# Modulation products of a two-block transformer step: k tiles outside, column groups of the array inside

## The reference

```python
cond_x = jax.nn.silu(c)
cond_c = jax.nn.silu(c_ctx)
for layer in range(DEPTH):
    mx = jnp.split((cond_x @ mod_w[layer] + mod_b[layer])[:, None, :], N_MOD, axis=-1)
    mc = jnp.split(cond_c @ mod_w[layer] + mod_b[layer], N_MOD, axis=-1)
    ...
```

## Time and profile before

| what | value |
|---|---|
| median of 3 runs | 3141.31 us (3138.47 to 3141.94) |
| span of the profiled execution | 3137.4 us |
| PE busy | 2995.0 us, 95% |
| DVE, ACT busy | 1347.2 us (43%), 1218.3 us (39%) |
| modulation products, line 902 | 576 records, 241.4 us together |
| loads of mod_w | 144 of 512 KB |

### The profile page before, as it was taken

The page is one execution under the profiler, slowest core; times in us unless marked ns, Lnnn a source line. Parts: engine busy times, 40 slices in busy tenths (PEclk is TensorE's granted clock), DMA queues, the critical chain, the costliest instruction groups (busy, mean ns, idle before and its releaser), DMA issues.

```text
span 3137.4 us, 44044 instructions
## 1 busy us (share of the span) xinstructions
PE 2995.0 (95%) x16870; PEld 2443.6 (78%) x16870; DVE 1347.2 (43%) x2147; ACT 1218.3 (39%) x1793; POOL 0.6 (0%) x6
## 2 busy tenths in 40 slices
PE   7999999999999999899998999899998999899998
PEld 6734989989338999888886568688876888687998
DVE  5521455556214555633334135433334333365555
ACT  5421635544115355533323234333323332245553
POOL 0000000000000000000000000000000000000000
PEclk9999999999999999999999999999999999999999
DMA  5575554654756455523232111232332223220454
GB/s 177 177 251 194 182 167 149 188 159 136 233 181 214 156 161 184 165 80 102 95 94 81 51 34 59 73 97 94 97 97 74 94 93 98 90 81 1 137 183 136
DMA packets 113830, 401.01 MB, mean 128 GB/s; under 512 B 12353, under 2 KB 15553, under 8 KB 113729
## 3 DMA queue, kind: packets, MB, share of 16 engines
q1 hardware_dynamic: 113728, 399.62, 39.6%
HBM read 398.52 MB, written 1.05 MB: 127 GB/s over the span
## 4 chain that ended last, share of the span: by engine, by line
PE 90%; DVE 4%; ACT 2%; DMA 2%; issue 1%; SPq 0%; DVEq 0%; ACTq 0%
PE psum L583 23%; PE psum L585 23%; PE psum L584 23%; PE psum L902 6%; PE psum L874 2%; DMA wring<-mod_w 2%; PE psum L938 1%; DVE arena L1521 1%; DVE HLO L1531 1%; PE psum L1039 1%; PE psum L1047 1%; ACT L1149 1%; PE psum L839 1%; PE psum L1004 0%; PE psum L972 0%
## 5 line engine op out<-in xcount | busy, mean ns | idle before, releaser
L583 PE MATMUL psum<-HHI,whi 128*128 128x256 f32 (+1 forms) x3456 | 1127.5, 326 | 64.5 <-DVE HLO L1531 39.7
L584 PE MATMUL psum<-HLO,whi 128*128 128x256 f32 (+1 forms) x3456 | 1114.6, 323 | 0.0
L585 PE MATMUL psum<-HHI,wlo 128*128 128x256 f32 (+1 forms) x3456 | 1113.9, 322 | 0.0
L1499 DVE TENSOR_TENSOR wlo<-wring,whi 128x1024 fp32r<-128x1024 f32 x590 | 709.1, 1223 | 489.9 <-ACT whi L1117 487.6
L1117 ACT ACTIVATE whi<-wring 128x1024 fp32r<-128x1024 f32 x590 | 607.6, 1054 | 480.6 <-PE psum L585 458.6
L583 PEld LDWEIGHTS psum<-HHI,whi 128*128 128x128 f32 x3456 | 664.3, 192 | 142.6 <-issue 64.9
L585 PEld LDWEIGHTS psum<-HHI,wlo 128*128 128x128 f32 x3456 | 666.1, 193 | 47.9
L584 PEld LDWEIGHTS psum<-HLO,whi 128*128 128x128 f32 x3456 | 666.8, 193 | 45.7 <-issue 0.5
L585 PE MATMUL psum<-HIDHI,wlo 128*128 128x256 f32 (+1 forms) x1056 | 356.9, 338 | 0.0
L583 PE MATMUL psum<-HIDHI,whi 128*128 128x256 f32 (+1 forms) x1056 | 356.4, 338 | 0.0
L584 PE MATMUL psum<-HIDLO,whi 128*128 128x256 f32 (+1 forms) x1056 | 355.3, 336 | 0.0
(11 more groups left out here) (272 smaller groups left out, 2063.3 us busy)
## 6 DMA issues: line engine op xcount, KB each, us to landing
wring<-ffn_in SPq DMA_DIRECT2D x264, 512.0 KB, 3.4
wring<-mod_w SPq DMA_DIRECT2D x144, 512.0 KB, 4.4
wring<-ffn_out SPq DMA_DIRECT2D x96, 448.0 KB, 3.4
wring<-w_proj SPq DMA_DIRECT2D x66, 512.0 KB, 3.4
wring<-w_gate SPq DMA_DIRECT2D x64, 512.0 KB, 4.3
wring<-ffn_out SPq DMA_DIRECT2D x48, 512.0 KB, 3.6
wring<-w_up SPq DMA_DIRECT2D x20, 512.0 KB, 3.4
wring<-w_out SPq DMA_DIRECT2D x16, 512.0 KB, 3.5
```

The costliest lines, as they stand in the source:

```text
L583: mm(out_, w[0], a[0], start=start, stop=False)
L584: mm(out_, w[0], a[1], start=False, stop=False)
L585: return mm(out_, w[1], a[0], start=False, stop=stop)
L1499: TTN(wlo[:, s, :], wring[:, raw_slot(tag, k), :], whi[:, s, :].bitcast(F32), ALU.subtract).then_inc(sem("weights_lo"), 1)
```

## The change

The two loops of the modulation products change places. Within the bank, the k tile runs outside and the column groups inside. A lot now holds, for one k tile, the blocks of two neighbouring column groups (a pair). `mod_place(j)` gives for lot j its bank filling b, its k tile and its pair: in the first four fillings 16 lots with two pairs for each k, in the fifth 8 lots with one pair. Each lot still issues two products of the same shapes, but they go to two different column groups, each with k as its place in the accumulation. The waits for a free bank and for a full bank move to the lots that are first and last in the new order. On the host, `mod_lots` lays the weights out to match; a lot has the same size, and the number of lots is the same.

```diff
+MOD_LOTS = 4 * MOD_G
...
+        def mod_place(j):
+
+            b = min(j // (2 * MOD_Q * 2), MOD_B - 1)
+            pairs = mod_rows(b) // 64
+            r = j - 16 * b
+            return b, r // pairs, r % pairs
...
-                for j in range(turn["lot"], min(turn["lot"] + n, 4 * MOD_G)):
-                    g, part = j // 4, j % 4
+                for j in range(turn["lot"], min(turn["lot"] + n, MOD_LOTS)):
+                    b, k, pair = mod_place(j)
+                    i = l * MOD_B + b
                     if (l, j) == (0, 0):
                         pe.wait_ge(*done("cond", 0))
-                    i, q = l * MOD_B + g // MOD_Q, g % MOD_Q
-                    if part == 0 and q == 0 and i >= 2:
+                    if k == 0 and pair == 0 and i >= 2:
 
                         pe.wait_ge(*done("mod_row", i - 2))
                     pe.wait_ge(*loaded(tag, 0, j))
                     w = raw_blocks(tag, j, 2, MOD_N)
                     for c in range(2):
-                        k = 2 * part + c
+
+                        q = 2 * pair + c
                         last = mm(psum[32 * q:32 * q + 32, RING + i % 2, :], COND[:, k, :], w[:, c, :],
                                   start=(k == 0), stop=(k == KT - 1))
                     lot_event(last, tag, ("rest", j))
...
             def mods_end():
-                mods_pe(4 * MOD_G)
+                mods_pe(MOD_LOTS)
...
-                act.wait_ge(*done("filled", ("lot", f"mod{l}", ("rest", 4 * (b * MOD_Q + m // 32) - 1))))
+                act.wait_ge(*done("filled", ("lot", f"mod{l}", ("rest", 16 * b + m // 8 - 1))))
...
     def mod_lots(w):
 
-        t = w.reshape(4, 2, P, MOD_G, MOD_N)
-        return asc(t.transpose(3, 0, 2, 1, 4)).reshape(4 * MOD_G, P, SLOT)
+        t = w.reshape(KT, P, MOD_G // 2, 2 * MOD_N).transpose(0, 2, 1, 3)
+        pairs = MOD_Q // 2
+        return np.concatenate([asc(t[:, pairs * b:pairs * b + pairs]).reshape(-1, P, SLOT) for b in range(MOD_B)])
```

## The result

The changed kernel takes **3101.6 us** (median of four runs, 3091.88 to 3107.16), and the kernel before, run on the same chip, 3141.6 us: a ratio of 0.986, with a 95% interval of 0.984 to 0.988. It is 40 us faster; 74 were forecast. A run that lies more than 1.5% above the fastest of its kernel is left out of a ratio, which here is one run of pair by pair (3119.2 us). The profiled execution is the slowest of the four, 3107.16 us, with a span of 3105.4. Its span is 32.0 us under the one of before, and both stretches together (169.5 and 172.4 us before, 155.1 and 154.6 after) account for 32.2 us. So nothing outside them has moved.

What follows compares the result with a forecast made beforehand. TensorE (PE) was taken to bound the kernel, loads close behind. A layer: -61.2 + 15.4 + 1 + 8 = -36.8 us, -73.6 for two; from span 3137.4 to 3063.8, median 3068 us, range 3020 to 3108.

Steps and rivals of the forecast that it cites:

- likeliest case: The forecast itself, all five terms together: 3068 us, own range 3045 to 3085, chance 0.42.
- First step: Modulation products: 72 lots a layer drop from 1.72 to 0.87 us each as two column groups overlap, -61.2 us.
- Second and third step: Modulation stretch: PE waits on lot loads (18.9 us), uncovered branch chains and the bank copy; together +15.4 us a layer.
- Fourth step: End of the stretch: gate loads queued behind the lots land a little closer to the end, +1 us a layer.
- Fifth step: Single lots between 8-row groups: more falls of the granted clock, 12 us in place of 4, +8 us a layer.
- second rival: Clock stays at 1.2 GHz through the single lots: +23.5 in place of +8 us a layer, 3099 us; chance 0.17.
- The first (no extra clock loss): Single lots: no extra clock loss and present falls go, -4 in place of +8 us a layer, 3044; chance 0.22.
- the loads at 1.9 us a lot: Modulation loads slower, 1.9 us a lot as in the stretch before: 16 us more a layer, 3100; chance 0.08.
- strict program order: Matmuls start and end strictly in program order, limiting overlap within a lot: 14 us more a layer, 3096; chance 0.03.
- no overlap: Column groups don't run beside each other within a lot: nothing changes, 3141 us; chance 0.03.
- The whole stretch at 1.2 GHz: All of the modulation stretch falls to 1.2 GHz because PE now waits in it: +40 us a layer, 3221; chance 0.05.
- one sign by which the prediction was to fail: The prediction was to fail if the clock fell outside the single lots; no size given.

Runs made afterwards that it cites:

- pair by pair: Changed kernel with the pair outside and the k tile inside in all bank fillings, so never four column groups at once; 3089.1 us, ratio 0.983.
- the two kernels at full height: 8-row products of the eight groups made 128 rows high, extra rows zero: in the changed kernel 3058.1 us, in the kernel before 3121.9 us.
- the kernel taken again: The changed kernel, unaltered, measured once more on another experiment's chip; 3093.6 us (3084.0 to 3111.13), ratio 0.984.
- the groups alone: Kernel before, its eight single lots moved from between the groups of 8-row products into the following run of 4; 3161.9 us, ratio 1.005.
- half loads: Changed kernel loading only the first half of each mod_w lot, the second column group multiplying stale weights; 3049.8 us, ratio 0.970.

## Why the prediction was right, and where it was short

The direction, the mechanism of the gain and the range held (3020 to 3108). The value, 3068, was 34 us too low, and the likeliest case's own range, 3045 to 3085, didn't hold the time. Step by step, a layer:

- **First step, 72 lots x 0.85 = -61.2 us: right in kind, too large.** Measured are -46.2 and -48.0. Some 7 us of the lots after and 3 of those before are low clock; without it, it is about -50 in this profile, and -48 between the two kernels at full height (116.8 and 118.2 to 70.1 and 68.4). Both ends of the subtraction were off. Before, I took 72 x 1.72 = 123.8, but 117 is right at full clock, since lots at the borders between column groups already overlapped; the row I argued from, 169.04, is such a border, and saves 1.7 us by itself. The prediction's own walk could have shown this: its 128.6 us of stretch less 20.2 of waits leave 108.4 us of work, 52.8 less than the 164.6 less 3.4 of falls, and not 61.2. After, 72 x 0.87 = 62.6 holds for lots that follow each other with two groups at once, and four at once take less (1.92 us for four lots). A lone lot costs 1.05, because nothing covers the end of its last record, and 32 lots of layer 0 came after a wait.
- **Second and third step, waits: +15.4 us, measured +16.9 and +16.1.** Waits of line 911 are 21.1 us, the copy 0.7; 18.9 and 0.7 were walked. Ahead of the single lots the loads came at 307 GB/s, a lot each 1.7 us on average; 1.55 was taken. The branch chains didn't show.
- **Fourth step, +1 us at the end:** nothing of that size is seen; the stretches alone make up the 32 us of span.
- **Fifth step, the clock, +8 us: the failed size.** It is the second rival's mechanism that happened in the profiled run: nearly all of the single lots at 1.2 GHz, in both layers. The stretch lost 20.2 us in layer 0 against the same code at full clock (47.0 and 26.8), where the falls of before had cost 3.4: +17, and +15 to +16 in layer 1. What the short falls outside it cost was not measured. I had put the mechanism at 17%, with its price at +23.5, and took a value between the ends because "the falls now are few". They were few because 1.72 us of a lot stood between two groups, and the change halves exactly this.

The two errors, some 11 and 9 us a layer, make up 40 of the 42 us by which the profiled run's span, 3105.4, lies over the forecast 3063.8. That the median lies near the second rival's 3099 is partly chance: with the first step at -50 this rival's sum is 3121, and with the clock at +17 in place of its +23.5 it is 3108, beside the profiled run's 3107. Of the other rivals, the loads at 1.9 us a lot, strict program order and no overlap are refuted by the rows above. The first (no extra clock loss) is what pair by pair did in its fastest run: 3067, not the 3044 I gave it, again by the first step. The whole stretch at 1.2 GHz did not come. But one sign by which the prediction was to fail did, in part: the clock fell outside the single lots, at 144.80 and 155.04 in layer 0, and its mean is 0.96 ahead of them, where it had been 1.00 (the 0.91 behind them is the end of the long fall). The waits on loads now reach 1.9 us. Nor did layer 0's stretch come down to the 125 to 140 us that were named, at 285 GB/s; it took 155.1, at 239.

What stays open: why the clock stays up in one run of a program and goes down in the next (in the profiled run of the changed kernel the clock fell among the groups; in layer 0 of the kernel taken again it fell after waits, 2.5 us ahead of them, and stayed down to their end), and which property of the 8-row products brings it down. Full height changes their rows and their length at once. These were not told apart.

## What to carry to other kernels

A saving computed as "count x (slot before - slot after)" should be made from the union of the busy time before, since part of the overlap may exist already, and with the lone item's full duration after wherever the item will arrive alone. If a stretch of odd-shaped products keeps its clock only thanks to the dense work mixed into it, then speeding up the dense work can take the clock away from both: price the whole stretch at 1.2 GHz, and look first for a form of the odd products that doesn't need the company. A time that differs by 1% between runs of one program calls for the granted clock of each run before it calls for an explanation.

## What the runs showed of the hardware that was not expected

- The granted clock fell to 1.2 GHz with PE busy for all of the time: 32.9 of 32.9 us at a mean of 0.56 in the groups alone. The Trainium skill, TensorE: Matmul & The Clock Gate, Part 1, ties a fall to an idle PE; this trace disagrees, while the changed kernel's short falls ahead of the single lots agree: in the 3 us before each of the three PE was busy for 1.3 us at most.
- The same products with 128 rows in place of 8, 120 of them zero, kept the clock at 1.00 and were shorter at full clock (a group 1.96 us, not 2.53).
- With the same single-lot code, the clock can be up for the whole stretch or down for nearly all of it, 26.8 or 47.0 us, or lie between (low for 30.9 of 41.2 us with half loads). A kernel's runs lay between 3067 and 3119 us, by the mean clock (0.981 to 0.964).
- Four 128x32 by 128x512 products in fp32, one for each column group, began within 25 ns, and 16 records took 1.92 us.
